# A fused attention and mixture-of-experts layer: two of an expert's six weight loads move to ScalarE's DMA queue

## What is computed

```python
h2 = rms_norm(x, norm2_w)
logits = h2 @ w_router + b_router            # 32 experts, top 4 per token
for e in range(32):
    u = h2[tokens_of_e] @ w1[e] + b1[e]      # w1[e]: 1024 x 2048
    gate, lin = split(u)
    gate = min(gate, 7); lin = clip(lin, -7, 7)
    a = gate * sigmoid(1.702 * gate) * (lin + 1)
    y = a @ w2[e] + b2[e]                    # w2[e]: 1024 x 1024
    acc[tokens_of_e] += y * routing_weight
```

## Time and profile before

| | |
|---|---|
| median of 3 runs | 1063.23 us |
| profiled execution | 1062.44 us, span 1060.7 us |
| granted TensorE clock, mean | 0.992 |
| PE busy | 1034.2 us, 98% of the span |
| DVE, ACT busy | 220.8 us, 116.9 us |
| moved by DMA | 424.69 MB, 423.25 of it on q1 |
| up projections (L1291) | 452.8 us in 2048 matmuls |
| down projections (L1304) | 227.2 us in 1024 matmuls |

### The profile page before, as it was taken

How to read it: one execution, slowest core, us unless ns; L and a number is a source line. 1 busy time by engine, 2 the same in 40 slices (tenths; PEclk the granted TensorE clock), 3 DMA queues, 4 the chain that set the end, 5 groups by cost and what they waited for, 6 DMA issues and landing times.

```text
span 1060.7 us, 12039 instructions
## 1 busy us (share of the span) xinstructions
PE 1034.2 (98%) x4961; PEld 419.8 (40%) x4961; DVE 220.8 (21%) x580; ACT 116.9 (11%) x219; POOL 0.2 (0%) x4
## 2 busy tenths in 40 slices
PE   9999999999999999999999999899999999999986
PEld 8888553333333333333333333233333333332332
DVE  2173432111111111111111111011111111111111
ACT  2131120000000000000000000000000000000002
POOL 0000000000000000000000000000000000000000
PEclk9999999999999999999999999899999999999998
DMA  9982979999999999999999999999999999999994
GB/s 321 370 353 80 334 289 399 431 427 426 429 427 426 430 427 426 429 425 428 428 427 427 428 427 428 426 426 428 429 426 428 428 426 429 427 426 431 426 426 192
DMA packets 45003, 424.69 MB, mean 400 GB/s; under 512 B 4904, under 2 KB 17456, under 8 KB 20112
## 3 DMA queue, kind: packets, MB, share of 16 engines
q1 hardware_dynamic: 44496, 423.25, 95.7%
q10 hardware_dynamic: 448, 0.59, 0.2%
HBM read 422.78 MB, written 1.05 MB: 400 GB/s over the span
## 4 chain that ended last, share of the span: by engine, by line
PE 91%; DMA 5%; DVE 2%; issue 1%; ACT 0%; another core or an unknown queue 0%; SPq 0%; DVEq 0%; ACTq 0%
PE PS L1291 40%; PE PS L1304 21%; PE PS L999 7%; PE PS L1274 5%; PE PS L1257 5%; DMA ring<-in_w 5%; PE PS L1180 3%; PE PS L1136 3%; PE PS L1319 2%; PE PS L1266 2%; PE PS L1244 1%; DMA ring<-in_w_in 1%; PE PS L1249 0%; PE PS L1402 0%
## 5 line engine op out<-in xcount | busy, mean ns | idle before, releaser
L1291 PE MATMUL PS<-ring,work 128*64 128x512 f32 x2048 | 452.8, 598 | 11.3 <-DMA ring<-in_w 7.1
L1291 PEld LDWEIGHTS PS<-ring,work 128*64 128x64 f32 x2048 | 144.4, 138 | 296.3 <-issue 281.0
L1304 PE MATMUL PS<-ring,work 128*64 128x512 f32 x1024 | 227.2, 596 | 1.6 <-DMA ring<-in_w 1.6
L1304 PEld LDWEIGHTS PS<-ring,work 128*64 128x64 f32 x1024 | 70.4, 137 | 155.5 <-issue 152.2
L891 DVE TENSOR_SCALAR work<-PS 128x512 f32<-128x512 f32 x32 | 22.1, 692 | 408.0 <-PE PS L1291 408.0
L999 PE MATMUL PS<-ring 128*128 128x256 f32 x384 | 85.6, 381 | 0.6 <-DMA ring<-in_w_in 0.6
L555 ACT ACTIVATE work<-work 128x512 f32<-128x512 f32 x32 | 20.2, 632 | 547.8 <-DVE work L891 547.8
L999 PEld LDWEIGHTS PS<-ring 128*128 128x128 f32 x384 | 72.0, 190 | 11.8 <-issue 1.3
L862 DVE TENSOR_TENSOR work<-PS,n2w 128x512 f32<-128x512 f32 x31 | 21.4, 692 | 229.1 <-PE PS L1266 229.1
L1274 PE MATMUL PS<-late,work 64*128 64x512 f32 x248 | 61.9, 616 | 0.7 <-ACT late L563 0.7
L1257 PE MATMUL PS<-resid,work 128*64 128x512 f32 x248 | 58.5, 592 | 0.0
(11 more groups left out here) (162 smaller groups left out, 363.7 us busy)
## 6 DMA issues: line engine op xcount, KB each, us to landing
ring<-in_w SPq DMA_DIRECT2D x189, 2048.0 KB, 32.3
ring<-in_w_in SPq DMA_DIRECT2D x11, 1024.0 KB, 12.0
ring<-in_w SPq DMA_DIRECT2D x5, 1024.0 KB, 7.8
ring<-in_w_out SPq DMA_DIRECT2D x4, 1024.0 KB, 12.5
ring<-in_w_in SPq DMA_DIRECT2D x2, 512.0 KB, 7.0
ring<-in_w SPq DMA_DIRECT2D x2, 512.0 KB, 46.2
ring<-in_consts SPq DMA_DIRECT2D x1, 800.0 KB, 11.8
resid<-in_x SPq DMA_DIRECT2D x2, 256.0 KB, 3.0
```

The source lines that it names most:

```text
L1291: last = mm(bank(v)[64 * half:64 * half + 64, :], gh[:, c, :], ring[:, 2 * d + c % 2, v * F + half * BANK:v * F + (half + 1) * BANK], star ...
L1304: last = mm(out[64 * half:64 * half + 64, :], aT_n[:, c, 64 * h:64 * h + 64], ring[:, 2 * d + c // 2, cols:cols + BANK], start=(h == 0 and ...
```

## The change

In steps 9 to 18 of the loop body (in its second turn steps 21 to 30), the chunks k = 1 and k = 3 are no longer issued by SyncE. ScalarE issues them, two steps ahead: in steps 7 to 16 (and 19 to 28), behind the sigmoid and ahead of `take_rows`. It waits for the same count of `chunk_used` as SyncE did for these chunks. The other four chunks of these steps stay with SyncE, in their order, and so do all chunks of the steps 0 to 8, 19, 20, 31 and 32. 40 loads of 2 MB move, 20 in each turn of the loop. The addresses, sizes and the semaphores that PE waits for stay.

```diff
+ACT_AHEAD, ACT_CHUNKS = 2, (1, 3)
...
             def step_loads(r, i, j):
                 for k in range(step_chunks(j)):
                     g = place_in_stream(j, k)
+                    if PEEL + ACT_AHEAD <= j < PEEL + UNROLL and k in ACT_CHUNKS:
+                        continue
...
+            def load_ahead(r, i, j):
+                for k in ACT_CHUNKS:
+                    e, d, g = local_expert(i, j), pair_of(j, k), place_in_stream(j, k)
+                    act.wait_ge(chunk_used, r * ROUND_CHUNKS + i * (UNROLL * STEP_CHUNKS) + (HEAD_CHUNKS + g - PAIRS + 1))
+                    act.dma_start(ring[:, 2 * d:2 * d + 2, :].rearrange("p a n -> p (a n)"),
+                                  w1_v[e, k, :, :]).then_inc(pair_full[d], 16)
+
             def expert_act(r, i, j):
                 n = r * E + local_expert(i, j)
 
                 if j < E:
                     act.wait_ge(gate_ready, n + 1)
                     nc.scalar.activation(s_sb, g_sb, ACT.Sigmoid, scale=ALPHA).then_inc(sig_ready, 1)
+                if PEEL <= j and j + ACT_AHEAD < PEEL + UNROLL:
+                    load_ahead(r, i, j + ACT_AHEAD)
                 if j < LAST:
                     take_rows(n + 1)
```

## The result

The changed kernel takes 1068.7 us (median of 6 runs, 1067.61 to 1071.51) against 1062.7 us of the kernel before (median of 6 runs): a ratio of 1.0055, 95% interval 1.0039 to 1.0071, which is 5.9 us slower (4.1 to 7.5). The forecast was slower, by 7.0 us, with 1070 as the time. The profiled execution took 1068.85 us, 6.4 us more than the one before (1062.44).

A forecast was written before the change was run, and what follows sets the result against it. The DMA stream was taken to set the end. ScalarE's and SyncE's issues, later issue and rate counted 0, delivery order +7.0 us: 1062.44 became 1069.4, given as 1070 us against the median, range 1062 to 1075.

The forecast's parts named there:

- The bound: Whole loop: the DMA stream needs 29.4 us a step, PE 27.4, so the stream sets the end.
- ScalarE's issues cost nothing: Behind ScalarE's sigmoid: two waits and two issues, 0.7 to 2.1 us, covered by 6.9 us before PE wants the copy: 0.
- The stream does not run dry: Step 7, where the stream is thinnest: k = 1 issued 8 us later still leaves loads queued: 0.
- Equal shares and overtaking: Two load queues share in halves, ScalarE's chunks land some 30 us early, SyncE's late: 6.6 to 7.5 us, chance 0.52.
- (29, 2) and the work behind it: Chunk k = 2 of step 29 lands three chunks, 14.7 us, late with 80.7 us of work behind: +7.0 us.
- No change: Rival on load order: chunks are served near their turn, so the end stays, 1062 to 1065 us; chance 0.22.
- Faster: Rival on the stream: two queues reach 431 GB/s without overtaking, -5.6 us, about 1057 us; chance 0.14.
- Slower by more: Rival: overtaking plus a rate 0.5% down or a clock drop after the last wait, +3.1 us, 1073 to 1076; chance 0.12.

The follow-up runs named there:

- slip3: Kernel before, all loads on SyncE's queue, k = 2 of loop step 17 issued three places late, behind k = 3, 4 and 5: 1.0084, +8.9 us.
- slip2: Kernel before, all loads on SyncE's queue, k = 2 of loop step 17 issued two places late, behind k = 3 and 4: 1.0024, +2.6 us.
- early: Changed kernel with k = 1 and 3 on ScalarE's queue only in loop steps 9 to 12, 16 moved loads: 0.9996 against the kernel before.
- late: Changed kernel with k = 1 and 3 on ScalarE's queue only in loop steps 15 to 18, 16 moved loads: 1.0072 against the kernel before.

## Why the prediction was right

**The bound.** Right. The stream stayed at 424 to 432 GB/s from the eighth slice to the 38th (in the kernel before to the 39th and not to the end: the last slice has 192, since the loads have landed by then), and every experiment that cost nothing ends in a transfer of some 49 us as the kernel before does.

**ScalarE's issues cost nothing.** Right; 0.91 us for the two lies within the 0.7 to 2.1. The wait between sigmoid and copy absorbed them; putting them behind the copy saved nothing that can be told. I had them issued 1.4 us after the projection's end; they go out 1.0 us after it, beside the sigmoid.

**The stream does not run dry.** Right for this change (427 GB/s over step 7). That it is thin there, as I had found, showed when two loads were put off by a whole step, and in the version with k = 0 and 1.

**Equal shares and overtaking.** Right, and the step on which all hangs. The forecast had halves, ScalarE's two loads in 19.6 us and SyncE's up to 55; measured were 53 to 47%, 19.4 and 54.0 us. The rule of the Trainium skill ("DMA: Bandwidth & Descriptors", Queues, rings and completion order) is that a DMA engine takes turns between the queues, a packet at a time. The trace agrees nearly: 252 packets of q1 and 212 of q10 from 958 to 974 us.

**(29, 2) and the work behind it.** Forecast to start at 977.5 to 978.4, with 80.7 us behind it and an end at 1058.2 to 1059.1. It starts at 977.16, a little earlier. PE's last group of matmuls, first before and then after, starts 6.1 us later, where the forecast had 6.6 to 7.5:

```profile
1050.53 1.88 PE L1274 MATMUL PS<-work 64*128 64x512 f32 x8
...
1056.64 1.88 PE L1286 MATMUL PS<-work 64*128 64x512 f32 x8
```

The chain puts PE's end at 1058.57, 81.4 us behind 977.16. But the 1051.6 from which the forecast counted is where ScalarE takes over in the chain of the kernel before, 0.8 us ahead of the end of its last group (1050.53 + 1.88). Counted in the same way the work behind (29, 2) is 80.6 us. The 7.0 us forecast are 1.1 more than the 5.9 measured and within its interval (4.1 to 7.5); the profiled executions differ by 6.4. That this order and not the second queue is the cause is shown by slip3 and slip2 (the same chunk put off on one queue) and by early and late (as many moved loads in two places).

**What was off.** The waits begin in step 21, not 22 to 24. I left the clock out because the waits would be short. Waits of 2.35 to 2.57 us did cost some clock: of the 32 matmuls behind the one at 916.43 the window shows

```profile
908.10:919.00 10.90, 7.09 (x32) 2.65 (x32) 1.48 (x6) 0.00 (x0) 0.00 (x0) 1.00 1.00 427
919.04:928.00 8.96, 8.96 (x34) 2.83 (x36) 0.18 (x1) 0.00 (x0) 0.00 (x0) 0.81 1.01 428
```

that is 8.72 us in place of 7.09. In the changed kernel this is hidden, since PE has to wait for (29, 2) anyway, and the wait for that one is 1.48 us and left the clock alone. Where the last wait was longer (1.99 us with k = 0 and 1, 2.08 with k = 2 and 3, 10.02 in slip2, 14.88 in slip3) it came through to the end, 1.7 to 2.5 us that none of the expectations had.

**The rivals.** "No change": the service was not in the order of issue. The Trainium skill ("DMA: Bandwidth & Descriptors", Rules for kernel authors) says that spreading DMAs over issuing engines gives no bandwidth and saves only issue time. Its half on bandwidth holds (427 GB/s on one queue and on two), but what decided was the order, about which that rule says nothing. "Faster" by a higher rate: no rate above the old one appeared. "Slower by more" through the clock: not in this kernel, but in four of the experiments.

## What to carry to other kernels

Loads of one stream on a second DMA queue did not move faster here, they moved ahead: the two full queues shared nearly in halves, so the short queue's loads landed early and the long queue's late by as many places as were passed. In a kernel where data arrives just in time, look for the last late load that still has less slack behind it than it is late; what stands behind it in work is the new end, and all earlier lateness is free. A load that is issued by an engine that itself depends on the consumer can close a ring, and then the consumer is tied to that load's landing in every step and can't build up slack.

## What the runs showed of the hardware that was not expected

TensorE's slower matmuls after a wait came sooner than I had thought. Over the chains of the changed kernel and of the versions with other pairs, after waits of up to 1.74 us the next matmuls ran at full speed (7.09 us for 32, 13.96 for 64); after waits of 1.99 to 4.81 us 1.5 to 1.7 us were lost (12.22 for 48 where 10.52 is usual, 8.78 for 32 where 7.09 is). The length of the wait alone does not decide it, though. One wait of 2.57 us in the version with the issues behind the copy cost nothing, and of seven waits of 1.95 to 2.29 us in the version one step ahead five cost nothing and two 1.7 us. In the late version 3.83 us cost 2.6 (6.21 for 16 where 3.65 is usual) and 3.47 us cost 2.9 (16.76 for 64), nearly as much as the 3.1 us behind the 4.20 us at the turn of the loop in the kernel before (such a turn cost 1.4 to 3.0 us in the other traces). After 10.02 and 14.88 us the loss was 2.5 and 1.9 us, less than behind some of the shorter ones. What else decides it stays open. In the windows shown, a loss of 1.6 us in 8.96 is what 3.3 us at the lower level of 1.2 GHz and the rest at 2.4 GHz would give, and that mixture has a mean of 0.82, close to the granted clock of 0.81.
